# The opening of a hybrid diffusion layer: modulation taken up in four feature pairs instead of two kinds

## The reference, cut to what matters

```
m = silu(cond) @ w_ada + b_ada            # cond: c (latent) or c_ctx (context); w_ada is 1024 x 6144
shift1, scale1, gate1, shift2, scale2, gate2 = split(m, 6)
h = rmsnorm(x) * norm1_g * (1 + scale1) + shift1
u = h @ w_in                               # q, k, v, z, beta, decay, attention and gate columns
```

## Time and profile before

| | us |
|---|---|
| median of 3 runs | 1416.37 |
| lowest, highest | 1414.94, 1416.93 |
| the profiled execution | 1417.62 |
| its span | 1415.8 |
| TensorE busy in the span | 1365.4 (96%) |
| VectorE, ScalarE, POOL busy | 814.1, 672.3, 223.6 |
| DMA moved | 142.92 MB, mean 101 GB/s |

### The profile page before, as it was taken

One profiled execution on the slowest core, in us unless ns is written; L12 is line 12 of the kernel. 1 busy time (PEld: TensorE's weight loads), 2 busy tenths in 40 slices (PEclk: granted clock), 3 DMA queues, 4 the chain that ended last, 5 costly groups with the idle time before them and its releaser, 6 DMA issues.

```text
span 1415.8 us, 26320 instructions
## 1 busy us (share of the span) xinstructions
PE 1365.4 (96%) x10442; PEld 1274.0 (90%) x10442; DVE 814.1 (57%) x1739; ACT 672.3 (47%) x1480; POOL 223.6 (16%) x189
## 2 busy tenths in 40 slices
PE   6999999999999999999998898999999999999998
PEld 3898989899998989999986776999999999999998
DVE  6466655756565565666435554757866433666422
ACT  4463736455373645537355554336655312555321
POOL 1010020202001020200020222000344002444100
PEclk7999999999999999999999999999999999999999
DMA  9542333142333324223416223532232322432232
GB/s 309 200 127 86 107 94 110 55 135 69 89 107 99 106 66 129 64 59 113 144 55 214 65 64 110 165 90 61 60 90 61 103 63 69 111 87 64 82 90 67
DMA packets 202304, 142.92 MB, mean 101 GB/s; under 512 B 9487, under 2 KB 187959, under 8 KB 201927
## 3 DMA queue, kind: packets, MB, share of 16 engines
q1 hardware_dynamic: 202183, 141.25, 33.7%
HBM read 125.19 MB, written 16.42 MB: 100 GB/s over the span
## 4 chain that ended last, share of the span: by engine, by line
PE 76%; DVE 10%; ACT 7%; issue 3%; SPq 2%; DMA 2%; POOL 1%; DVEq 0%; ACTq 0%
PE ps L1182 23%; PE ps L1700 15%; PE ps L1737 11%; PE ps L1481 7%; PE ps L1408 2%; PE ps L1635 2%; PE ps L1352 1%; DVE tri L2585 1%; PE ps L1415 1%; PE ps L1256 1%; PE ps L1427 1%; DVE tri L2626 1%; DVE W_r L2579 1%; PE ps L1426 1%; PE ps L1358 1%
## 5 line engine op out<-in xcount | busy, mean ns | idle before, releaser
L1182 PE MATMUL ps<-hT_r,WAH_r 128*128 128x320 f32 x912 | 229.0, 332 | 5.6 <-ACT zs L2033 2.4
L1182 PE MATMUL ps<-xT_r,WAH_r 128*128 128x320 f32 x912 | 208.0, 309 | 0.0
L1182 PEld LDWEIGHTS ps<-hT_r,WAH_r 128*128 128x128 f32 x912 | 145.5, 190 | 24.8 <-issue 11.5
L1182 PEld LDWEIGHTS ps<-xT_r,WAH_r 128*128 128x128 f32 x912 | 153.2, 188 | 0.0
L1182 PE MATMUL ps<-hT_r,W_r 128*128 128x320 f32 x592 | 134.5, 310 | 0.0
L1737 PE MATMUL ps<-a_part,W_r 128*128 128x320 f32 x704 | 132.4, 310 | 0.4 <-DVE naT_r L2910 0.4
L3127 POOL TENSOR_TENSOR gm<-sqkq,dt 128x1280 f32<-128x1280 f32 x8 | 23.5, 2936 | 574.6 <-DVE Xc L2621 502.6
L1737 PEld LDWEIGHTS ps<-a_part,W_r 128*128 128x128 f32 x704 | 110.2, 188 | 0.6 <-DVE naT_r L2910 0.6
L1700 PE MATMUL ps<-t_big_r,W_r 128*128 128x320 f32 x380 | 107.2, 310 | 0.5 <-ACT naT L2288 0.5
L1700 PE MATMUL ps<-b_part,W_r 128*128 128x320 f32 x456 | 101.4, 309 | 1.4 <-DVE oT_r L2897 1.4
L1182 PEld LDWEIGHTS ps<-hT_r,W_r 128*128 128x128 f32 x592 | 99.6, 190 | 0.0
(11 more groups left out here) (436 smaller groups left out, 3267.2 us busy)
## 6 DMA issues: line engine op xcount, KB each, us to landing
oT<-in_ffn_w SPq DMA_DIRECT2D x44, 512.0 KB, 5.3
W<-in_w_in SPq DMA_DIRECT2D x36, 512.0 KB, 4.0
WAH<-in_w_ada SPq DMA_DIRECT2D x18, 1024.0 KB, 6.7
naT<-in_w_in SPq DMA_DIRECT2D x24, 512.0 KB, 4.2
oT<-in_ffn_w SPq DMA_DIRECT2D x16, 704.0 KB, 4.6
ext_dram<-naT SPq DMA_DIRECT2D x28, 320.0 KB, 4.1
GCB<-gc_dram SPq DMA_DIRECT2D x7, 640.0 KB, 4.6
W<-in_w_pa SPq DMA_DIRECT2D x8, 512.0 KB, 3.9
```

The source lines that it names most:

```text
L1182: m = e.matmul(ps[:, bank + b, 0:n], w[:, k, :], x[:, k, a:a + n], start=k == 0 and i == 0, stop=k == KD - 1 and i == 2, skip_group_check= ...
```

## The change

The four groups are divided by features. Group n now holds the shift and the scale columns of blocks 2n and 2n+1: 256 columns of each, still 2 MB in total. It arrives as two transfers, one for each kind, with rows of 1 KB where there were rows of 2 KB, and is multiplied by 16 matmuls of 256 columns instead of 8 of 512. `gains(n)` is called four times, each for two blocks. All groups are turned into one PSUM bank, so a transpose waits until VectorE has read the one before (`ada_out`).

Around that the orders of all engines are written anew:

- TensorE: after group 0 and its transposes, for n = 0 to 3: the q strip of blocks 2n and 2n+1, group n+1, logits of 2n, transposes of group n+1, logits of 2n+1, the k strip of both blocks.
- VectorE: four blocks are normed first, then gains(0), the exact form of blocks 0 and 1, the q strip's small part, the small parts of blocks 0 and 1, that of the logit weights, two more normed blocks, gains(1), and so on in pairs. The last pair is taken one block after the other. The v strip's small part comes after all blocks.
- ScalarE: copies out a group before it rounds the pair that depends on it.
- SyncE: group 0, q strip, group 1, the nine small transfers, k strip, groups 2 and 3, v strip.
- POOL: the three memsets of tile tri also wait for the last block of `h`.

The whole diff, without empty lines:

```diff
@@ -399 +399,2 @@
-        ADA_ORDER, ADA_BANK = (0, 2, 1, 3), (6, 7, 7, 6)
+        WP_OF, ROW_BANK, TURNED = (0, 2, 1, 3), (1, 6, 6, 6), 7
+        QW = 2 * P
@@ -825,3 +826,4 @@
-            def ada_in(i):
-                for j in range(2):
-                    e.dma_start(WP[i][:, 4 * j:4 * j + 4, :], w_ada[:, 4 * j:4 * j + 4, i * 4 * P:(i + 1) * 4 * P]).then_inc(ld_wp[i][j], 16)
+            def ada_in(n):
+                i = WP_OF[n]
+                for s in range(2):
+                    e.dma_start(WP[i][:, :, s * QW:(s + 1) * QW], w_ada[:, :, s * D + n * QW:s * D + (n + 1) * QW]).then_inc(ld_wp[i][s], 16)
@@ -834 +835,0 @@
-            ada_in(2)
@@ -836 +837 @@
-            opening_in("k")
+            ada_in(1)
@@ -845 +846,2 @@
-            ada_in(1)
+            opening_in("k")
+            ada_in(2)
@@ -1166,4 +1168,10 @@
-                i = ADA_ORDER[n]
-                if n == 3:
-                    e.wait_ge(ada_row, 3)
-                ada_rows((1, 2, 6, 6)[n], 4 * P, WP[i], ld_wp[i], 16).then_inc(ada_mm, 1)
+                i, bank = WP_OF[n], ROW_BANK[n]
+                if n >= 2:
+                    e.wait_ge(ada_row, n)
+                for s in range(2):
+                    e.wait_ge(ld_wp[i][s], 16)
+                    for k in range(KD):
+                        j = k % 4
+                        m = e.matmul(ps[32 * j:32 * j + 32, bank, s * QW:(s + 1) * QW], csT[:, k, :], WP[i][:, k, s * QW:(s + 1) * QW],
+                                     start=k < 4, stop=k >= 4, skip_group_check=True)
+                m.then_inc(ada_mm, 1)
@@ -1173,0 +1182,2 @@
+                if n:
+                    e.wait_ge(ada_out, 2 * n - 1)
@@ -1175 +1185 @@
-                    m = e.transpose(ps[:, ADA_BANK[n], c * P:(c + 1) * P], arow0[:, n % 2, c * P:(c + 1) * P], IDN)
+                    m = e.transpose(ps[:, TURNED, c * P:(c + 1) * P], arow0[:, n % 2, c * P:(c + 1) * P], IDN)
@@ -1207 +1216,0 @@
-            ada_group(1)
@@ -1209 +1217,0 @@
-            ada_select(1)
@@ -1212,14 +1220,12 @@
-            for k in range(KD):
-                if k == 2:
-                    ada_group(2)
-                if k == 3:
-                    ada_group(3)
-                e.wait_ge(h_done, k + 1)
-                opening_mm("q", k)
-                if k == 3:
-                    ada_select(2)
-                    ada_select(3)
-                for held in {0: (), 1: (0, 1), 2: (), 3: (2, 3)}.get(k, (k,)):
-                    logits_mm(held)
-                for held in {0: (), 1: (0, 1), 2: (), 3: (2, 3), 6: (), 7: (6, 7)}.get(k, (k,)):
-                    opening_mm("k", held)
+            for n in range(4):
+                for k in (2 * n, 2 * n + 1):
+                    e.wait_ge(h_done, k + 1)
+                    opening_mm("q", k)
+                if n < 3:
+                    ada_group(n + 1)
+                logits_mm(2 * n)
+                if n < 3:
+                    ada_select(n + 1)
+                logits_mm(2 * n + 1)
+                for k in (2 * n, 2 * n + 1):
+                    opening_mm("k", k)
@@ -1793 +1799 @@
-                e.activation(arow0[:, n % 2, :], ps[:, (1, 2, 6, 6)[n], :], ACT.Copy).then_inc(ada_row, 1)
+                e.activation(arow0[:, n % 2, :], ps[:, ROW_BANK[n], :], ACT.Copy).then_inc(ada_row, 1)
@@ -1814 +1819,0 @@
-            ada_out_row(1)
@@ -1817 +1821,0 @@
-            opening_big(wbas[:, :, 0, :], wba[:, :, :], ld_ba, 16 * 9)
@@ -1819 +1823 @@
-            opening_big(OPENING_BIG["k"], W[:, slot["k"], :, :], ld_w["k"], 16)
+            opening_big(wbas[:, :, 0, :], wba[:, :, :], ld_ba, 16 * 9)
@@ -1821,2 +1825,4 @@
-            for k in range(2, KD // 2):
-                round_h(k)
+            ada_out_row(1)
+            opening_big(OPENING_BIG["k"], W[:, slot["k"], :, :], ld_w["k"], 16)
+            round_h(2)
+            round_h(3)
@@ -1823,0 +1830,2 @@
+            round_h(4)
+            round_h(5)
@@ -1826,2 +1834,2 @@
-            for k in range(KD // 2, KD):
-                round_h(k)
+            round_h(6)
+            round_h(7)
@@ -2410 +2418,2 @@
-            for k in range(KD):
+            def normed(k):
@@ -2413 +2422 @@
-            def gains(half):
+            def gains(n):
@@ -2415 +2424 @@
-                a, z = 4 * half, 4 * half + 4
+                a, z = 2 * n, 2 * n + 2
@@ -2417 +2426,3 @@
-                b = cols[:, B_ADA:B_ADA + 16].rearrange("p (s k) -> p s k", s=2)[:, :, a:z].unsqueeze(3).to_broadcast([P, 2, 4, 2])
+                b = cols[:, B_ADA:B_ADA + 16].rearrange("p (s k) -> p s k", s=2)[:, :, a:z].unsqueeze(3).to_broadcast([P, 2, 2, 2])
+                e.wait_ge(ada_sel, n + 1)
+                parts = ps[:, TURNED, :].rearrange("p (s k g r) -> p s k r g", s=2, k=2, g=4)
@@ -2419,4 +2430 @@
-                    n = 2 * half + j
-                    e.wait_ge(ada_sel, n + 1)
-                    parts = ps[:, ADA_BANK[n], :].rearrange("p (k g r) -> p k r g", k=4, g=4)[:, :, 0:2, :]
-                    m = e.tensor_reduce(both_rows[:, j, :, :], parts, AX.X, ALU.add)
+                    m = e.tensor_reduce(both_rows[:, j, :, :], parts[:, j, :, 0:2, :], AX.X, ALU.add)
@@ -2424 +2432 @@
-                e.wait_ge(ada_out, 2 * half + 1)
+                e.wait_ge(ada_out, 2 * n + 1)
@@ -2426,3 +2434,3 @@
-                e.wait_ge(ada_out, 2 * half + 2)
-                e.scalar_tensor_tensor(gain1[:, a:z, :], mods[:, 8 + a:8 + z, :], 1.0, cols[:, N1 + a:N1 + z].unsqueeze(2).to_broadcast([P, 4, 2]), ALU.add, ALU.mult).then_inc(gain_done, 1)
-                e.wait_ge(gain_done, half + 1)
+                e.wait_ge(ada_out, 2 * n + 2)
+                e.scalar_tensor_tensor(gain1[:, a:z, :], mods[:, 8 + a:8 + z, :], 1.0, cols[:, N1 + a:N1 + z].unsqueeze(2).to_broadcast([P, 2, 2]), ALU.add, ALU.mult).then_inc(gain_done, 1)
+                e.wait_ge(gain_done, n + 1)
@@ -2441,0 +2450,2 @@
+            for k in range(4):
+                normed(k)
@@ -2444,0 +2455 @@
+            exact_h(1)
@@ -2447,2 +2457,0 @@
-            exact_h(1)
-            opening_small(wbas[:, :, 1, :], wba[:, :, :], wbas[:, :, 0, :], 2)
@@ -2450 +2459,4 @@
-            opening_kind("k", 3)
+            opening_small(wbas[:, :, 1, :], wba[:, :, :], wbas[:, :, 0, :], 2)
+            normed(4)
+            normed(5)
+            gains(1)
@@ -2452,0 +2465 @@
+            opening_kind("k", 3)
@@ -2454,0 +2468,2 @@
+            normed(6)
+            normed(7)
@@ -2457,2 +2472,10 @@
-            opening_kind("v", 4)
-            gains(1)
+            gains(2)
+            exact_h(4)
+            exact_h(5)
+            small_h(4)
+            small_h(5)
+            gains(3)
+            exact_h(6)
+            small_h(6)
+            exact_h(7)
+            small_h(7)
@@ -2462,5 +2485 @@
-            exact_h(4)
-            for k in range(KD // 2, KD):
-                if k < KD - 1:
-                    exact_h(k + 1)
-                small_h(k)
+            opening_kind("v", 4)
@@ -3100,0 +3120 @@
+            e.wait_ge(h_done, KD)
```

6 lines of the change are left out of this document (3 added, 3 removed).

## The result

The changed kernel took 1423.60 us (median of 6, 1422.54 to 1425.35) against 1417.31 (median of 6, 1414.94 to 1419.34) for the kernel before: ratio 1.0045, 95% interval 1.0034 to 1.0057. A second set gave 1423.07 and 1.0050 (1.0037 to 1.0063). The forecast of 1418.8 and the top of its range, 1422.4, were too low. A small part of that is the kernel before: the forecast started from its median of 1416.37, and over the whole set it is 1417.31. The profiled execution took 1425.35 us, span 1423.6.

What follows compares the result with a forecast made beforehand. The opening was taken to hang on the last modulation group's load. An earlier start, three rounds of 8.4 us and an unhidden last block move its end from 59.3 to 61.7: 1416.37 plus 2.4 gives 1418.8 us, range 1414.3 to 1422.4.

Steps and rivals of the forecast that it cites:

- The loop and its parts: Opening: each pair of blocks needs one round through all engines, 8.4 us at the high clock.
- q block 7: End of opening: with the last pair no longer interleaved, q block 7 starts 2.5 us after q block 6.
- the rival that it falls in every round: Opening: gaps of 1.4 us lower TensorE's clock each round, +3.4 us, 1422.2 us; chance 0.18.
- First wrong term: the rows: Opening loads: 1 KB rows cost nothing; at 300 GB/s group 0 alone would be late, by 1.5 us.
- the first q block: Start of opening: TensorE begins q block 0 at 25.2 us, where it began at 30.5 before.
- the cold stretch: First round: low clock, first k strip ends at 37.9 or, cold, 39.4 us; 38.6 taken for q block 2.
- a cold q pair: Opening, TensorE: two q blocks at the low clock take 3.2 us instead of 1.76; counted in the first round.
- the forecast's own range: 1417.2 us with the clock kept high in the first round's gap, to 1420.3 with cold k strip, q pair and groups of 2.1.
- the forecast's rival with the clock high throughout: Opening: clock high from the start; q pair, group and k strip shorten, ending at 58.7, 1415.7 us; chance 0.12.
- Behind the opening I change nothing: After the opening: logits, q and k strips end in the same order and nearly the same distance from its end.
- a difference behind the first 62 us: Sign of being wrong: a time difference that arises after the opening.

Runs made afterwards that it cites:

- The fillers: Changed kernel plus 11 TensorE matmuls whose results nobody reads, five ahead of q block 0 and six ahead of the first k strip: 1421.91 us, 1.0042.
- before again: The kernel before, unchanged, measured and profiled a second time: 1416.66 us, 0.9995.
- v strip moved: Kernel before with only the v strip's rounding and small part moved behind all blocks: 1415.54 us, 0.9993.
- last pair interleaved: Changed kernel with VectorE making the exact forms of blocks 6 and 7 first, then both small parts: 1419.85 us, 1.0025.
- both halves waited for: Kernel before with TensorE waiting for both halves of each group before its first product, transfers and products as before: 1417.42 us, 1.0007.
- groups ahead: Changed kernel with groups 2 and 3 ahead of their round's q blocks on TensorE, their transposes behind the first of these: 1420.41 us, 1.0030.
- and 1 KB rows: Kernel before with group transfers in 1 KB rows and both halves waited for, products of 512 columns as before: 1419.66 us, 1.0013.
- mended order: Changed kernel with groups 1 to 3 ahead of the q blocks, last two blocks interleaved, k strip's small part before exact forms 2 and 3: 1414.75 us, 0.9993.
- POOL early: Changed kernel with POOL's three memsets no longer waiting for the last block of h, released as early as before: 1425.12 us, 1.0054.
- 1 KB rows and narrow products: Kernel before with each group in two transfers of 256 columns and sixteen matmuls of 256, division and orders as before: 1421.02 us, 1.0026.
- narrow products: Kernel before with sixteen matmuls of 256 columns per group and both halves waited for, 2 KB rows as before: 1420.72 us, 1.0022.
- 64 fillers: Kernel before with 64 idle products of 32 columns added on TensorE ahead of q block 0: 1438.40 us, 1.0142.
- the pairs with the strip issued early: SyncE issues the w_pa strip ahead of its attention wait and cached rows: changed kernel 1420.55 and 1419.99 us, kernel before 1412.74 and 1412.20 us.

## Why the prediction was wrong

**What it had right.** The loop and its parts. Rounds three and four begin 8.48 us apart (49.19 and 57.67) where 8.4 was said; q block 7 follows 2.35 later (2.5); from q block 6 to the end it takes 6.3 (6.3). A group of the new shape takes 1.86 from 42.37 to the logits. No group after the first waited for its load; the gaps of 1.18, 0.88 and 1.19 us left the clock at 1.00, so the rival that it falls in every round did not come. The Trainium skill, "TensorE: Matmul & The Clock Gate", section "HAM oscillation", says that a wait inside every step can throttle the array again. Its own case has longer waits than these, and here, with gaps of about 1 us in the later rounds, that did not come. It was the one gap of 2.84 us, ahead of the first k strip, after which the clock fell, as the rows had made likely.

**First wrong term: the rows.** The forecast let rows of 1 KB cost nothing, by one window at 127 us with 379 GB/s. In the opening they moved at 348, so group 0 was ready at 17.80 instead of 16.98. All of that passed through: the first q block came at 26.00, not 25.2. Some of the 0.8 is chance. Over all profiles group 0's second half starts at 17.06 to 17.90 in the twelve with rows of 1 KB and at 16.63 to 17.41 in the eight with rows of 2 KB, 0.6 apart in the mean. With the rows alone in the old kernel this term is 0.9 us at group 0 and 1.9 at the mark. The forecast had the path (at 300 GB/s it gave 1.5 us, which would go through) and set its price at zero.

**Second: the cold stretch.** The clock was said to be open between 37.9 and 39.4 and taken in the middle. It stayed low to 31.4 us (0.65 from 30 to 32) and fell again at 38.2 (0.55 from 38 to 40). Block 2 came at 39.61, 1.0 late: 0.8 from the rows and 0.3 from a cold q pair (3.5 instead of 3.2), less 0.1. Then the second round was 9.58 instead of 8.4. Its q pair took 2.76 instead of 1.76 (39.61 to 42.37), the remaining 6.82 are near 6.64. So the fall was counted for the k strip, but not for the q blocks behind it; a cold q pair stood only in the upper end of the forecast's own range. The k strip itself took 2.48 (37.13 to 39.61), just the middle that was guessed between 1.76 and 3.2. The fillers put the price of both low stretches in the opening at about 3.0 us, and the forecast's rival with the clock high throughout had 3.0.

The ends of the forecast's own range do not follow from its terms, either. A k strip that ends at 37.9 is 0.7 earlier than 38.6 and gives 1418.1, not 1417.2. A cold k strip (+0.8), a cold q pair (+1.4) and two groups of 2.1 (+0.5) give 1421.5, not 1420.3.

The two make the 2.2 us between 61.7 and 63.9: 0.8 start of group 0, 0.3 first q pair, 1.0 second, 0.1 small terms. By themselves they would have left the time within the range: 1418.8 + 2.2 is 1421.0.

**Third: "Behind the opening I change nothing".** The time behind the opening was set at no change, without a row that showed it, though a difference behind the first 62 us was named as a sign of being wrong. That sign came: +1.9 us in the first set, +3.1 in the second. It is this term that takes the time out of the range: 1421.0 and 1.9 are 1422.9, and the median of before rose by 0.9 besides. All rests, in us:

| without more TensorE products | rest | with them | rest |
|---|---|---|---|
| before again | -0.8 | changed kernel | +1.9, +3.1 |
| v strip moved | +0.4 | last pair interleaved | +1.1 |
| both halves waited for | +0.1 | groups ahead | +3.4 |
| and 1 KB rows | -0.9 | mended order | +2.6 |
| | | POOL early | +2.1 |
| | | fillers for the clock | +6.0 |
| | | 1 KB rows and narrow products | +2.1 |
| | | narrow products | +1.7 |
| | | 64 fillers | +2.4 |

The four kernels without added products on TensorE have rests of -0.9 to +0.4, the ten sets with them +1.1 to +6.0. For the pairs with the strip issued early the difference is 1.9 and 3.3. Each rest is uncertain by 1.3 to 2.5 us from its ratio's interval and by about 0.5 from its opening, so it is the two groups that stand apart and not each rest.

A check that sets nothing from different executions against each other is the time from the mark to the end within one profiled execution (span less mark). It is 1351.8 to 1354.6 us in the five profiles without added products and 1353.6 to 1358.5 in the ten with them. The means are 3.0 apart, but the ranges overlap (mended order 1353.6, rows and products 1354.1, last pair interleaved 1354.3). For the pairs with the strip issued early the changed kernel has 2.5 us more in one and 0.7 less in the other. So the rest goes with the added products in the mean, and not in every execution.

This is a correlation. What the added instructions do to the later stages is not shown. In the profiles the distance grows between 750 and 876 us, by idle time and low clock at changing places, and the one place that I tested, the wait at 800 us, costs all kernels about the same 4 us. Which mechanism takes the time behind the opening stays open. The loss of 6.4 us is then 4.2 to 4.6 in the opening, shown, and about 2 behind it, which goes with the narrow products and whose cause is not shown.

The direction of the forecast was right, and so was the mechanism for the opening, a loop that gives back more than the earlier start brings. The size was off, and with 0.38 for slower against 0.50 for the same it put the weight on the wrong side of 2.8 us.

## What to carry to other kernels

When a load is cut so that each piece serves sooner, price the shorter rows at the very place where the first consumer waits, not from a quiet window elsewhere: the first piece has no slack. When one wait becomes several, write out the loop through the engines and take out of it what needn't be there: pulling the next group ahead of the q pair, interleaving the last pair and moving the k strip's small part up together took 7.6 us off the opening. Such a gain is none until the total shows it: that opening was 3.6 us shorter than before's, and the time was the same. And look for a transfer that sits in a queue behind a wait that it doesn't need: moving one such issue brought 3 to 5 us in all three kernels tried.

## What the runs showed of the hardware

- HBM rows of 1 KB into 128 partitions moved at 346 to 349 GB/s, rows of 2 KB at 384 to 389, in the same stretch of the opening, 14 to 16 us. As an estimate by the Trainium skill, "DMA: Bandwidth & Descriptors", section "Why small descriptors are slow (HBM only)", with three cycles more for each row of 32-byte beats, the ratio would be 0.957 (32/35 against 64/67); measured was 0.90.
- The clock fell at about 800 us after idle times of 2.27, 2.41 and 2.84 us and stayed high after 2.43 and 2.68 (and 2.01 in the mended order) in other executions: the length of the gap alone does not tell.
- The clock can also fall in dense work, in one execution and not in the next. In the first profile of before TensorE is busy throughout 75 to 85 us and the clock is 0.75 and 0.91 over the two halves; in the second it is 1.00 in both, and the second is 1.5 us ahead from there on.
- Holding the clock up paid about 3.0 us at the opening's end. What of it reaches the program's end, these sets cannot tell.
- A TensorE product of 32 columns with a 128x128 f32 weight tile took 0.40 us at the low clock; two of 320 columns with rounded tiles take 0.53 together there. Narrow f32 products are not small ones.
